# First expert stage of a two-block transformer: experts in pairs, plain float32 products

## What is computed

```python
g_sel = argmax(h @ w_rg + b_rg)                     # one of 4 groups
top_v, top_i = top_k(e_logit[g_sel], 2)             # two of the group's 8 experts
gate = softmax(top_v) * g_p
for each picked expert e:                           # w_gate, w_up: 1024 x 512, w_down: 512 x 1024
    out += gate_e * ((silu(h @ w_gate[e]) * (h @ w_up[e])) @ w_down[e])
x = x + out
```

## Time and profile before

| | us |
|---|---|
| median of 3 runs | 2308.96 (2308.01 to 2310.91) |
| span of the profiled execution | 2305.0 |
| TensorE busy (matmul) | 2257.6 (98%) |
| TensorE weight loads | 1850.2 (80%) |
| DVE busy | 1805.8 (78%) |
| ACT busy | 1484.0 (64%) |
| loads over the whole span | 617.54 MB, mean 268 GB/s |

### The profile page before, as it was taken

One profiled execution on the slowest core, in us unless ns is written; L12 is line 12 of the kernel. 1 busy time (PEld: TensorE's weight loads), 2 busy tenths in 40 slices (PEclk: granted clock), 3 DMA queues, 4 the chain that ended last, 5 costly groups with the idle time before them and its releaser, 6 DMA issues.

```text
span 2305.0 us, 30582 instructions
## 1 busy us (share of the span) xinstructions
PE 2257.6 (98%) x12386; PEld 1850.2 (80%) x12386; DVE 1805.8 (78%) x1915; ACT 1484.0 (64%) x1493; POOL 25.0 (1%) x35
## 2 busy tenths in 40 slices
PE   9999999999999999999999999999999999999997
PEld 7678888888888887877888787888888888888886
DVE  8766678888888886786554677788898888989886
ACT  6555457777767776565434656577677666777765
POOL 1000000000000000000000010000000000000000
PEclk9999999999999999999999999999999999999999
DMA  9754449999999996525655531599999989999991
GB/s 225 202 146 146 165 157 344 366 356 370 366 358 363 356 366 228 178 79 189 199 164 201 166 130 41 178 351 359 366 358 368 357 300 353 355 368 356 370 340 73
DMA packets 281506, 617.54 MB, mean 268 GB/s; under 512 B 31880, under 2 KB 130440, under 8 KB 243984
## 3 DMA queue, kind: packets, MB, share of 16 engines
q1 hardware_dynamic: 279952, 611.85, 76.6%
q10 hardware_dynamic: 1408, 3.67, 0.4%
HBM read 612.34 MB, written 1.05 MB: 266 GB/s over the span
## 4 chain that ended last, share of the span: by engine, by line
PE 87%; DVE 8%; ACT 4%; issue 1%; POOL 0%; DVEq 0%; ACTq 0%; POOLq 0%
PE ps L589 14%; PE ps L585 14%; PE ps L586 14%; PE ps L575 10%; PE ps L577 10%; PE ps L576 10%; DVE ring_parts L612 2%; PE ps L2385 2%; ACT high_parts L608 1%; PE ps L2001 1%; PE ps L2003 1%; PE ps L2008 1%; DVE arena L1491 1%; PE ps L2334 1%; PE ps L733 1%
## 5 line engine op out<-in xcount | busy, mean ns | idle before, releaser
L612 DVE TENSOR_TENSOR ring_parts<-ring,high_parts 128x2048 fp32r<-128x2048 f32 (+1 forms) x574 | 1283.2, 2276 | 117.4 <-ACT high_parts L608 116.4
L608 ACT CAST high_parts<-ring 128x2048 fp32r<-128x2048 f32 (+1 forms) x574 | 1079.6, 1898 | 172.8 <-PE ps L589 86.2
L577 PE MATMUL ps<-high_parts,arena_parts 128*128 128x512 f32 (+1 forms) x1112 | 437.3, 393 | 0.0
L585 PE MATMUL ps<-high_parts 128*128 128x512 f32 x912 | 361.3, 396 | 0.0
L586 PE MATMUL ps<-high_parts 128*128 128x512 f32 x912 | 357.8, 392 | 0.0
L575 PE MATMUL ps<-high_parts,arena_parts 128*128 128x512 f32 x632 | 249.9, 395 | 2.0 <-DVE ring_parts L612 1.0
L589 PE MATMUL ps<-ring_parts,high_parts 128*128 128x512 f32 x912 | 248.9, 395 | 0.0
L576 PE MATMUL ps<-ring_parts,arena_parts 128*128 128x512 f32 x632 | 248.9, 394 | 0.0
L577 PEld LDWEIGHTS ps<-high_parts,arena_parts 128*128 128x128 f32 x1112 | 209.1, 188 | 48.0
L585 PE MATMUL ps<-high_parts,hT_parts 128*128 128x512 f32 (+1 forms) x576 | 229.2, 399 | 0.8 <-ACT arena L1311 0.8
L589 PEld LDWEIGHTS ps<-ring_parts,high_parts 128*128 128x128 f32 x912 | 171.5, 188 | 38.7
(11 more groups left out here) (583 smaller groups left out, 2535.3 us busy)
## 6 DMA issues: line engine op xcount, KB each, us to landing
ring<-in_moe_w SPq DMA_DIRECT2D x248, 1024.0 KB, 5.3
ring<-in_w_gate SPq DMA_DIRECT2D x64, 1024.0 KB, 6.4
ring<-in_w_up SPq DMA_DIRECT2D x64, 1024.0 KB, 6.2
ring<-in_w_down SPq DMA_DIRECT2D x64, 1024.0 KB, 6.2
ring<-in_w_in SPq DMA_DIRECT2D x104, 256.0 KB, 4.6
ring<-in_ffn_w SPq DMA_DIRECT2D x44, 512.0 KB, 5.0
ring<-in_w_in SPq DMA_DIRECT2D x20, 1024.0 KB, 5.2
ring<-in_moe_w SPq DMA_DIRECT2D x32, 512.0 KB, 5.1
```

Of the source, the lines that this page charges most:

```text
L577: return pe.matmul(dst, a_lo, b_hi, start=False, stop=last, skip_group_check=True)
L585: pe.matmul(dst, x_hi, w_hi, start=first and i == 0, stop=False, skip_group_check=True)
L608: act.copy(high_flat(p), raw_flat(p)).then_inc(upper, 1)
L612: dve.tensor_tensor(raw_flat(p, ring_parts_flat), raw_flat(p), f32(high_flat(p)), ALU.subtract).then_inc(split, 1)
```

## The change

- Tokens are bucketed by pair of experts (16 pairs), in 64 slots each, not by group in 128. Two pairs form one bucket of 128 slots, so there are 8 buckets of 2 steps; a step has two experts, one for each pair, and 12 pieces.
- Each product of a step is made twice, once for each expert, into the lower and the upper 64 partitions of the same PSUM bank, with 64 columns of weights. Both are plain float32 products, straight from the ring: no casts and no subtractions for this stage, neither for the weights nor for the gathered rows nor for the hidden rows. Gather and scatter stay split. TensorE frees two slots at a time (`then_inc(used, 2)`).
- The gather runs twice, for four buckets of 128 slots each, since the selection matrix covers 512 slots.
- The router finds the two experts ahead of the count, since the places are now counted by pair. `gates1_dve` keeps only what follows the exponential.
- The early splits of the first two pieces beside the projection before the stage go.
- The loop for what is left starts beyond 64 tokens in a pair, and has two passes.

The diff, cut to its core:

```diff
+PAIRS, HALF = NE1 // 2, P // 2
...
+        def plan_pairs(name, w1, w3, w2, gain_row):
+
+
+            f = weights_of(w1, w3, w2)
+            f.name, f.number, f.gain_row = name, 1, gain_row
+            f.subs, f.e, f.cap, f.passes = PAIRS, 2, HALF, 2
+            f.buckets = PAIRS // 2
+            f.base, f.plan = dict(moe_before), []
+            rows = [w2[e].rearrange("(p c) n -> p c n", p=P) for e in range(NE1)]
+            for b in range(f.buckets):
+                for j in range(2):
+                    st = Step()
+                    st.bucket, st.j, st.experts = b, j, (4 * b + j, 4 * b + 2 + j)
+                    f.plan.append(st)
+
+            def down(st):
+                return [[new_piece([(0, PIECE, rows[e][:, c:c + 2, :])]) for e in st.experts] for c in (0, 2)]
+
+            for s, st in enumerate(f.plan):
+                st.no = s + 1
+                st.up = [[new_piece([(0, PIECE, w[e][:, c:c + 4, :])]) for e in st.experts] for w in (f.w1, f.w3) for c in (0, 4)]
+                if s:
+                    f.plan[s - 1].down = down(f.plan[s - 1])
+            st.down = down(st)
...
+        moe1 = plan_pairs("moe1", d["w_gate"][0], d["w_up"][0], d["w_down"][0], d["norm2_g"])
...
+            if f is moe1:
+                lot = [p for st in f.plan for pair in st.up + st.down for p in pair]
+            else:
+                lot = [p for st in f.plan for p in st.up] + [p for st in f.plan for p in st.down]
             stream(sp, sorted(lot, key=lambda p: p.n))
...
-            over = eng.value_load(most[0:1, c:c + 1], min_val=0, max_val=S) >= P + 1
+            over = eng.value_load(most[0:1, c:c + 1], min_val=0, max_val=S) >= f.cap + 1
...
-                    act.wait_ge(used, pieces_of["out_1"][1].n + 1)
-                    split_high(act, moe1.plan[0].up[0])
...
-                if i == n_ab + 13 and phase:
-                    split_low(dve, moe1.plan[0].up[0])
...
+            groups, hot, off = r_log[:, :, 0:N_GROUPS], r_oh1[:, :, 0:N_GROUPS], r_oh2[:, :, 0:N_GROUPS]
             all_of(first_max(dve, groups, N_GROUPS, r_c[:, 11], r_c[:, 12], hot))
+            dve.tensor_scalar(r_c[:, 9], r_c[:, 11], -1.0, None, ALU.mult).then_inc(sig("router_group"), 1)
+            vstep(dve, dve.tensor_scalar(off, hot, BIG, -BIG, ALU.mult, ALU.add))
+            for t in range(NT):
+                e8, m8 = [v.rearrange("p (g k) -> p g k", g=N_GROUPS) for v in (r_log[:, t, N_GROUPS:36], r_em[:, t])]
+                ins = dve.tensor_tensor(m8, e8, off[:, t].unsqueeze(2).to_broadcast([P, N_GROUPS, PER_GROUP]), ALU.add)
+            vstep(dve, ins)
+            all_of(top_two(dve, r_em, NE1))
+            vstep(dve, dve.tensor_tensor(r_em, r_oh1, r_oh2, ALU.add))
+            vstep(dve, dve.tensor_reduce(r_hit, r_em.rearrange("p t (b k) -> p t b k", k=2), AX, ALU.max))
             dve.drain().then_inc(sig("routed"), 1)
-            dve.tensor_scalar(r_c[:, 9], r_c[:, 11], -1.0, None, ALU.mult).then_inc(sig("router_group"), 1)
             place_dve(dve, moe1)
...
+        pair_rows = [MX.take(KC, TOGETHER * P) for _ in range(2)]
...
+        def pair_rows_ready(eng, r, c):
+            eng.wait_ge(sig(("moe_rows_upper", "moe_rows")[c % 2]), KC // 2 * r + c // 2 + 1)
+
+        def pairs_pe(pe, f):
...
+                for c in range(2, KC):
+                    if c >= 3:
+                        pair_rows_ready(pe, r, c - 3)
+                    for t in range(NT):
+                        chunk(c, t)
...
+            def turn(st):
+                pe.wait_ge(sig("moe_hid"), st.no)
+                if st.no > 1:
+                    pe.wait_ge(sig("moe_hidT"), st.no - 1)
+                for c in range(4):
+                    mm = pe.transpose(ps[:, TURN, c * P:(c + 1) * P], m_hid[:, c::4], ident[:])
+                mm.then_inc(sig("moe_turned"), 1)
...
+            def up(st, h):
+                r, q = divmod(st.bucket, TOGETHER)
+                bank, c0 = (GATE, UP)[h // 2], 4 * (h % 2)
+                w = [v.rearrange("p (c n) -> p c n", n=512) for v in pieces_in(st.up[h])]
+                for i in range(4):
+                    if h < 2 and st.bucket % TOGETHER == 0:
+                        pair_rows_ready(pe, r, c0 + i)
+                    for a in range(2):
+                        rows = slice(a * HALF, (a + 1) * HALF)
+                        mm = pe.matmul(ps[rows, bank, :], pair_rows[r][:, c0 + i, q * P + a * HALF:q * P + (a + 1) * HALF], w[a][:, i, :],
+                                       start=(c0 + i == 0), stop=(c0 + i == KC - 1), skip_group_check=True)
+                mm.then_inc(used, 2)
...
+            def down(st, h):
+                if h == 0:
+                    pe.wait_ge(sig("moe_hidT"), st.no)
+                    if st.j == 0 and st.bucket:
+                        pe.wait_ge(sig("moe_y"), st.bucket)
+                w = [v.rearrange("p (c n) -> p c n", n=D) for v in pieces_in(st.down[h])]
+                ends = st is f.plan[-1] and h == 1
+                for i, half in ((0, 0), (1, 0), (0, 1), (1, 1)) if ends else ((0, 0), (0, 1), (1, 0), (1, 1)):
+                    c = 2 * h + i
+                    for a in range(2):
+                        rows = slice(a * HALF, (a + 1) * HALF)
+                        mm = pe.matmul(ps[rows, half, :], pair_hidT[:, c, rows], w[a][:, i, half * 512:(half + 1) * 512],
+                                       start=(st.j == 0 and c == 0), stop=(st.j == 1 and c == 3), skip_group_check=True)
+                    if ends and (i, half) == (1, 0):
+                        mm.then_inc(sig("moe_half_done"), 1)
+                mm.then_inc(used, 2)
...
+            held = None
+            for s, st in enumerate(f.plan):
+                b = st.bucket
+                if s == len(f.plan) - 3:
+                    ahead = pe.mark_branch_hint_location()
+                if s == 0:
+                    gather(0)
+                if s > 1:
+                    turn(held)
+                if held:
+                    pe.wait_ge(sig("moe_silu"), held.no)
+                up(st, 0)
+                if s == 1:
+                    pe.wait_ge(*ended("moe1_gates"))
+                    gates(0)
+                up(st, 1)
+                if s == 1:
+                    turn(held)
+                if st.j and b:
+                    scatter(b - 1, 0)
+                if st.j == 0 and b == TOGETHER - 1:
+                    for c in (KC - 2, KC - 1):
+                        pair_rows_ready(pe, 1, c)
+                    gates(1)
+                if held:
+                    pe.wait_ge(sig("moe_hid"), held.no)
+                up(st, 2)
+                if st.j and b:
+                    scatter(b - 1, 1)
+                up(st, 3)
+                if st.j and b:
+                    scatter(b - 1, 2)
+                if st.j and b % TOGETHER == 0:
+                    if b:
+                        scatter(b - 1, 3)
+                    turn_sel(b // TOGETHER)
+                if held:
+                    down(held, 0)
+                    if st.j and b % TOGETHER:
+                        scatter(b - 1, 3)
+                    down(held, 1)
+                if st.j and b == TOGETHER - 2:
+                    gather(1)
+                held = st
+            turn(held)
+            down(held, 0)
+            down(held, 1)
+            rest_pe(pe, f, ahead)
+            for q in range(4):
+                scatter(f.buckets - 1, q)
...
+            def hidden(st):
+                act.wait_ge(sig("moe_turned"), st.no)
+                if st.no > 1:
+                    act.wait_ge(used, f.plan[st.no - 2].down[1][1].n + 1)
+                act.copy(pair_hidT.rearrange("p c n -> p (c n)"), ps[:, TURN, :]).then_inc(sig("moe_hidT"), 1)
...
+            def silu(st):
+                act.wait_ge(used, st.up[1][1].n + 1)
+                if st.no > 1:
+                    act.wait_ge(sig("moe_hid"), st.no - 1)
+                r, q = divmod(st.bucket, TOGETHER)
+                if st.no > 1:
+                    act.wait_ge(sig("moe_gates"), r + 1)
+                else:
+                    act.wait_ge(sig("moe_rows_upper"), KC // 2)
+                scale = m_gate[:, 12 * r + 3 * q + 2:12 * r + 3 * q + 3] if st.no > 1 else m_rstd
+                act.activation(m_sg, ps[:, GATE, :], ACT.Silu, scale=scale).then_inc(sig("moe_silu"), 1)
...
+            rest_act(act, f, ahead)
+            split_until(act, "act", group_in[0], 1)
+            act.wait_ge(sig("moe_scattered"), 4 * (f.buckets - 1))
+            act.wait_ge(*ended("moe_half_done", 1, 0))
+            act.copy(m_yh[:, 0:512], ps[:, 0, :]).then_inc(sig("moe_half_upper"), 1)
+            act.wait_ge(used, held.down[1][1].n + 1)
+            act.copy(m_yh[:, 512:D], ps[:, 1, :]).then_inc(sig("moe_y_upper"), 1)
+            split_until(act, "act", group_in[0], 2)
...
+            def product(st):
+                dve.wait_ge(used, st.up[3][1].n + 1)
```

(28 more changed lines are left out.)

325 lines of the change are left out of this document (231 added, 94 removed).

## The result

The changed kernel takes 2230.63 us (median of 4 runs, 2228.87 to 2232.36) where the kernel before takes 2308.49 (2307.66 to 2310.91): 0.9662 of it, with a 95% interval of 0.9648 to 0.9675. That is 78 us saved. The forecast was 2245.8 us, 63 us saved, in a range of 2224 to 2295. Its sign and its mechanism were right, and one term was mis-sized.

A forecast was written before the change was run, and what follows sets the result against it. TensorE was taken to bound the first expert stage, with loads becoming the bound after the change. Its end at 830.0 instead of 893.2 saves 63.2 us: 2305.0 - 63.2 + 4.0 = 2245.8 us, range 2224 to 2295.

The forecast's parts named there:

- TensorE bounds the stage of before, the loads don't yet: First expert stage before the change: TensorE busy 567.6 of 569.0 us; loads, 2.86 us each, issued at TensorE's pace.
- rival A: First expert stage: DMA engines already at their limit, a load still costs 2.86 us, time 2293 us; chance 0.16.
- TensorE's step of 23.4 us: First expert stage, two experts: 24 overlapping pairs at 0.86 us, plus transposes, scatter and changes of shape.
- The load at 2.60 us: First expert stage: a 1 MiB load costs 2.60 us once loads are the bound, within 2.49 to 2.75.
- The start: Router ahead of the stage: 4.0 us of DVE operations and 1.7 of slow clock; first product 338.2, first slots 341.6.
- The end: End of the stage: 6.8 us of cast and subtraction, then 3.3 to the first turn of x, at 830.0.
- After the stage: Next stage begins with about four loads landed instead of a full ring: costed at nothing, without that cover 2.6 us.
- The sum: Whole kernel: stage end 893.2 to 830.0 saves 63.2 us, giving 2245.8 us.
- B: First expert stage: TensorE's clock falls as it waits for loads; all at 1.2 GHz gives 2522 us; chance 0.05.
- C: First expert stage: the two halves don't overlap for 512 columns, a step takes 44.1 us, time 2479 us; chance 0.03.

The follow-up runs named there:

- half the bytes: The changed kernel with only the first half of each load's columns read in the first expert stage, all products kept: 2137.55 us.

## Why the prediction was right, and where it was off

- **TensorE bounds the stage of before, the loads don't yet:** right. The kernel before with two of three products (and most of DVE's subtractions of the weights left out) reached 421 GB/s. The argument from landing times (6.3 us in the stage, 5.1 alone) was the one that carried; the share of 0.99, which spoke for rival A, was misleading.
- **TensorE's step of 23.4 us:** right. With half the bytes, 16 steps and the gather took 379.4 us instead of 383. Full overlap of the halves, taken from eight small records of 128 columns, holds for 512 columns too: a group of four pairs takes 3.65 us to its end, and four groups in a row (half the bytes, 525.75 to 539.70) 13.95, 0.87 a pair.
- **The load at 2.60 us:** this is the term that was mis-sized. Issue of the first load at 342.05, last one used at 802.36: (802.36 - 342.05 - 5.1) / 182 = 2.50 us, at the lower edge of the 2.49 to 2.75 that I had allowed. The 0.10 us too much, 182 times, are 18 us, more than the whole error of 14.7 in the span (15.2 in the median, 2245.8 to 2230.63). I had two stretches of 5 us, 421 and 403 GB/s, called both picked maxima and took the lower. The upper one was the steady rate: no stretch of 50 us of the stage exceeds 422, though single stretches of 5 us go from 415 to 429. In the trace of before nothing told the two apart: 421 stood alone, and the next highest stretches of 5 us were 403 and 401. Those probably had a queue that ran empty in between, which I haven't shown. The Trainium skill's 408.7 GB/s (DMA: Bandwidth & Descriptors, section iDMA fabric) would have given 2.57 us and is below what the trace shows as well. Nearer is what its page HBM Reference, section Specifications, says of a core that streams alone, about 425 GB/s; the trace, 421, agrees. I had weighed only the share of 358 given there and on the DMA page, which by that page holds with the neighbour core streaming.
- **The start:** the first product was foreseen at 338.2 and came at 338.35, the first free slot at 341.6 and 342.05. That it is so near is partly luck: the gather began 4.9 us later than before where I had put 4.0, and it lost 0.9 us to the clock where I had put 1.7. Other kernels here with the same router have their first product between 337.7 and 340.4. The 16 DVE operations ahead of the count did leave TensorE idle for 4.66 us, and the granted clock did fall. It fell earlier and for longer than taken (0.51 for 6.9 us from 324.4, not for 3.4 us at the gather), over spare transposes too.

```profile
326.00 0.63 PE L1763 MATMUL ps<-r_pairs,causal_up 128*128 128x32 f32 x2 [4.66 <-DVEq L1908]
...
326.87 2.16 PE L782 MATMUL ps<-ident 128*128 128x128 f32 x9
328.68 0.78 PE L2752 MATMUL ps<-arena_parts 128*128 128x512 f32 x1
...
338.35 7.09 PE L2830 MATMUL ps<-ring,arena 128*64 128x512 f32 x32
...
342.05 3.76 SPq L535 DMA_DIRECT2D ring<-in_w_gate  x3
```

- **The end:** foreseen 10.1 us from the last landing to the next turn, measured 11.0 (802.36 to 813.37). The chain foreseen is there, line by line: ACT's cast of the next stage's load, DVE's subtraction of it, then that of the half result. It hid a second one, the branch, which no row of before shows as long. And the clock fell once more, for 6.8 us from 809.1, which I hadn't foreseen: the scatters take 0.43 us a record in it instead of 0.23.

```profile
802.36 3.65 PE L2845 MATMUL ps<-ring,arena 128*64 128x512 f32 x16 [1.28 <-DMA ring<-in_w_down]
...
804.92 1.90 ACT L657 CAST high_parts<-ring 128x2048 fp32r<-128x2048 f32 x1 [7.54 <-DMA ring<-in_w_in]
...
806.85 2.29 DVE L661 TENSOR_TENSOR ring_parts<-ring,high_parts 128x2048 fp32r<-128x2048 f32 x1 [14.36 <-ACT high_parts L657]
...
809.06 0.68 DVE L3034 TENSOR_TENSOR arena_parts<-ps,arena_parts 128x512 fp32r<-128x512 f32 x1
...
809.79 0.80 PE L2812 MATMUL ps<-arena_parts 128*128 128x512 f32 x1 [3.78 <-DVE arena_parts L3034]
...
813.37 1.91 PE L798 MATMUL ps<-ident,x 128*128 128x128 f32 x8
```

- **After the stage:** foreseen at no cost. The stage ends 79.8 us earlier (893.21 to 813.37) and the span is 77.9 shorter. The 1.9 us between are differences of a few us in both directions in the second block, among them a fall of the clock at 1290 that the kernel before doesn't have. I haven't traced them further.
- **The sum:** 18 us less for the loads, 0.4 more at the first slot, 0.9 more at the end, 1.9 more behind it: 14.7, which is the difference of the spans, 2241.8 to 2227.1.
- **The rivals:** A fell by the run on the kernel before. B didn't come about in the changed kernel, whose clock stayed full through the pauses that I had feared. It came true in its mechanism where half of the products were left out, and there the loads hid it. C fell: with alternation the overlap is full, and even without it the halves overlap in part. The range of 2224 to 2295 held the time, near its lower end; of its 71 us the upper 22 were A, the rest the price of a load.

## What to carry to other kernels

A busy share of the DMA engines near 1 doesn't say that they are at their limit; the time from issue to landing does. If it is hardly above that of a lone load, the queue is nearly empty and there is rate to gain. How much, one trace may not tell: here the fastest stretch of 5 us was the right rate and the next ones, which agreed with each other, were too low. A run of the kernel before with some of TensorE's work left out gives the rate directly. When a stage is bound by its loads, look at when loads can't be issued at all: memory for four more of them was worth 8.7 us here, while halving the arithmetic was worth 4.6. An idle time put down to "issue" behind a branch is worth a look at the queue's own records.

## What the runs showed of the hardware that I had not expected

- Three loads of 1 MiB in flight keep the rate at 421 GB/s; two give 374 to 402 from 390 on, with runs from 2259 to 2342 us.
- Products of 64 columns on different halves of TensorE overlap though four of one half stand in a row ahead of those of the other: 5.42 us for a group of eight that is broken off on both sides, 4.21 for each of four in a row (16.84 / 4), 3.65 when alternated.
- The same branch took 0.49 us in one kernel and 5.81 in another that differs from it only by 40 transposes some 480 us earlier, and between 0.39 and 6.2 over all of them. The cause is open.
- With half of the products left out, the granted clock spent 157 of 450 us at its low level, in pieces, and the loads hid it.
